# Group 0 of a hybrid decoder step: all v, all u, all q, with four u buffers and later side loads

## The reference, cut to what matters

```python
h = rmsnorm(x, g_mix)
u, q, f, v, og, ga, gb = split(h @ w_in)
# branch A: causal pooling, windows 2, 4, 8, 16 on four groups of 128 channels
pooled = (window_sum(u, w) / count) - u           # one w for each channel group
ya = (pooled @ w_pool * pool_scale) @ w_a
# branch B: gated linear recurrence, 4 heads of 128 x 128
f = lb + (1 - lb) * sigmoid(f);  k = 1 - f
S_t = diag(f_t) S_{t-1} + k_t outer v_t;  o_t = S_t^T silu(q_t)
yb = (rmsnorm(o) * silu(og)) @ w_b
m = sigmoid(ga) * ya + sigmoid(gb) * yb;  x = x + m @ w_out
x = x + relu(rmsnorm(x) @ w_up)^2 @ w_down;  y = rmsnorm(x)
```

## Time and profile before

| | |
|---|---|
| median of 3 runs | 926.98 us (924.71, 926.98, 990.6) |
| the profiled execution | 923.54 us |
| its span, from the first to the last instruction of the slowest core | 922.0 us (core 2) |
| spans of the eight cores | 917.0 to 922.0 us |
| PE busy | 875.5 us, 95% |
| DVE, ACT, POOL busy | 420.2, 360.3, 121.2 us |
| chain that ended last | PE 85%, issue 4%, ACT 3%, DMA 3%, DVE 3%, POOL 2% |
| `arena<-w_in` on that chain | 3% |

### The profile page before, as it was taken

How to read it: one execution, slowest core, us unless ns; L and a number is a source line. 1 busy time by engine, 2 the same in 40 slices (tenths; PEclk the granted TensorE clock), 3 DMA queues, 4 the chain that set the end, 5 groups by cost and what they waited for, 6 DMA issues and landing times.

```text
span 922.0 us, 14969 instructions; the slowest of 8 cores (917.0 to 922.0 us)
## 1 busy us (share of the span) xinstructions
PE 875.5 (95%) x4935; PEld 456.1 (49%) x5017; DVE 420.2 (46%) x692; ACT 360.3 (39%) x636; POOL 121.2 (13%) x190
## 2 busy tenths in 40 slices
PE   4699999999999999999999999999999999999997
PEld 3366754454444434455444444444444444688443
DVE  4555463866757764853643222442134421233122
ACT  4553534666275634652133321332223321333222
POOL 3112420035101430233210000000000000000000
PEclk9799999999999999999999999999999999999999
DMA  9999624047513465996999632400511002200022
GB/s 188 214 156 151 121 86 160 12 132 188 165 55 104 118 168 184 178 150 85 165 212 181 102 92 92 92 1 1 137 49 44 0 4 89 71 2 1 25 68 72
DMA packets 81480, 94.90 MB, mean 103 GB/s; under 512 B 27741, under 2 KB 62173, under 8 KB 81388
## 3 DMA queue, kind: packets, MB, share of 16 engines
q0 software_dynamic: 23984, 30.41, 23.6%
q1 hardware_dynamic: 57420, 63.52, 23.5%
HBM read 92.35 MB, written 26.11 MB: 128 GB/s over the span
## 4 chain that ended last, share of the span: by engine, by line
PE 85%; issue 4%; ACT 3%; DMA 3%; DVE 3%; POOL 2%; DVEq 0%; SPq 0%; ACTq 0%; POOLq 0%
PE ps L585 47%; PE ps L1322 24%; PE ps L597 9%; ACT arena L563 3%; DMA arena<-w_in 3%; PE ps L1028 1%; POOL arena L566 1%; DVE arena L666 1%; DVE arena L566 1%; DMA arena<-meta 1%; PE ps L742 0%; PE ps L880 0%; PE ps L1320 0%; PE ps L619 0%; PE ps L759 0%
## 5 line engine op out<-in xcount | busy, mean ns | idle before, releaser
L585 PE MATMUL ps<-arena 128*128 128x512 bf16 (+2 forms) x2677 | 493.7, 340 | 19.7 <-DMA arena<-w_in 8.0
L585 PEld LDWEIGHTS ps<-arena 128*128 128x128 bf16 x2720 | 262.4, 98 | 226.2 <-issue 29.5
L563 ACT ACTIVATE arena<-ps 128x512 f32<-128x512 f32 (+7 forms) x328 | 191.2, 597 | 307.2 <-PE ps L585 224.2
L563 ACT ACTIVATE arena<-arena 128x1024 bf16<-128x1024 f32 (+7 forms) x235 | 154.3, 669 | 247.8 <-DVE arena L1336 166.9
L1322 PE MATMUL ps<-arena 128*128 128x512 bf16 x1003 | 220.6, 379 | 1.2 <-issue 0.2
L566 DVE TENSOR_TENSOR arena<-arena 128x512 bf16<-128x512 f32 (+6 forms) x214 | 146.8, 692 | 133.4 <-ACT arena L563 125.7
L1322 PEld LDWEIGHTS ps<-arena 128*128 128x128 bf16 x1024 | 100.0, 98 | 121.4 <-issue 1.3
L566 DVE TENSOR_TENSOR arena<-ps,arena 128x512 f32<-128x512 f32 (+5 forms) x155 | 108.4, 716 | 86.2 <-PE ps L585 19.5
L597 PE MATMUL ps<-arena 128*128 128x512 bf16 (+2 forms) x467 | 107.6, 381 | 1.3 <-DMA arena<-w_in 0.4
L1336 DVE SCALAR_TENSOR_TENSOR arena<-ps,arena 128x1024 f32<-128x1024 f32 (+2 forms) x18 | 22.0, 1223 | 152.5 <-PE ps L1322 138.1
L566 POOL TENSOR_TENSOR arena<-arena 128x512 f32<-128x512 bf16 (+7 forms) x78 | 76.0, 982 | 82.6 <-DMA arena<-sth 29.4
(11 more groups left out here) (97 smaller groups left out, 248.4 us busy)
## 6 DMA issues: line engine op xcount, KB each, us to landing
arena<-xp SPq DMA_DIRECT2D x32, 512.0 KB, 6.5
arena<-w_in POOLq DMA_DIRECT2D x9, 1024.0 KB, 23.5
x1d<-arena SPq DMA_DIRECT2D x16, 512.0 KB, 4.9
arena<-w_up POOLq DMA_DIRECT2D x8, 1024.0 KB, 12.7
arena<-x1d SPq DMA_DIRECT2D x16, 512.0 KB, 4.7
y_p<-arena SPq DMA_DIRECT2D x15, 512.0 KB, 3.3
arena<-w_down POOLq DMA_DIRECT2D x5, 1024.0 KB, 24.9
h2d<-arena SPq DMA_DIRECT2D x16, 256.0 KB, 4.1
```

The costliest lines, as they stand in the source:

```text
L563: P.add("act", lambda h: h.activation(out=out, in_=in_, func=func, **kw), reads=reads, writes=writes)
L585: i = h.matmul(ps[:, bb, 0:m], lhsT=wfn(k), rhs=rfn(k, c, m), start=(k == 0), stop=(k == K - 1))
```

## The change

It does five things.

1. In group 0 the twelve units run as v x4, u x4, q x4 (`seq`), where they were v, v, u, v, u, v, q, q, u, q, u, q. Groups 1 to 3 keep the old order.
2. Group 0 has four u buffers; the third and fourth lie on two of the x buffers.
3. The `stp` loads move out of `load_rest1` into `load_rest2` and wait for the eviction of `u_og(0)`. The three early x tiles wait for the load of `w_a` (and for the readers of the third and fourth u buffer). `w_a` goes ahead of ga0 in POOL's queue, and `fold_wa2` goes two units forward, ahead of the last of the first four gb units.
4. The normalisation of the next group's x and the reloads of the present x go 5 later in group 0.
5. Pooling times: in group 0 the third u at 5.1 and 6.1 and the fourth at 6.2 and 7.2 after their units, in groups 1 to 3 the third at 5.5 and 6.5 (was 1.5 and 2.5), the fourth at 4.6 and 5.6 (was 3.2 and 4.1). The recurrence tiles start at 15.6 + 3.35 t, where it was 15.7 + 3.4 t.

```diff
+        r_u += [region(o_x + 4096 * i, 2176) for i in (1, 2)]
+        uext += [view(o_x + 4096 * i, 544, F32) for i in (1, 2)]
@@
         def load_rest1():
             P.add("sp", lambda h: h.dma_start(out=wpf, in_=w_poolT), reads=r_T1[1].bufs, writes=r_wpf.bufs, dma=True)
+
+        def load_rest2():
             for j in range(2):
-                P.add("sp", lambda h, j=j: h.dma_start(out=stp_sb[0:120, j, :], in_=stp[j * 120:(j + 1) * 120, :]), writes=[r_stp.bufs[j]], dma=True)
+                P.add("sp", lambda h, j=j: h.dma_start(out=stp_sb[0:120, j, :], in_=stp[j * 120:(j + 1) * 120, :]), reads=r_sog.bufs[0:1], writes=[r_stp.bufs[j]], dma=True)
@@
-            a, b = ((4.9, 4.9), (3.4, 3.5), (1.5, 2.5), (3.2, 4.1))[gg]
+            a, b = (((5.0, 5.0), (4.6, 4.6), (5.1, 6.1), (6.2, 7.2)) if g == 0 else ((4.9, 4.9), (3.4, 3.5), (5.5, 6.5), (4.6, 5.6)))[gg]
@@
-                    i = m % 2
+                    i = m if g == 0 else m % 2
@@
+                A(19.5, load_rest2)
                 for t in range(3):
-                    A(12.1 + t, lambda t=t: early.update({t: xload(x_rows(1, t), 128, r_T1[3].bufs)}))
-                A(26.2, lambda: [fold_wa2(gg) for gg in range(4)])
+                    A(20.1 + t, lambda t=t: ([activate(r) for r in r_x[1:3]] if t == 0 else None, early.update({t: xload(x_rows(1, t), 128, r_wa.bufs)})))
+                A(24.1, lambda: [fold_wa2(gg) for gg in range(4)])
@@
-                z = 15.7 + e + 3.4 * t
+                z = 15.6 + e + 3.35 * t
@@
-            for fn, i in ((u_v, 0), (u_v, 1), (u_u, 0), (u_v, 2), (u_u, 1), (u_v, 3), (u_q, 0), (u_q, 1), (u_u, 2), (u_q, 2), (u_u, 3), (u_q, 3)):
+            seq = [(u_v, t) for t in range(4)] + [(u_u, m) for m in range(4)] + [(u_q, m) for m in range(4)]
+            for fn, i in seq if g == 0 else ((u_v, 0), (u_v, 1), (u_u, 0), (u_v, 2), (u_u, 1), (u_v, 3), (u_q, 0), (u_q, 1), (u_u, 2), (u_q, 2), (u_u, 3), (u_q, 3)):
@@
-                for t, z in enumerate((7, 11, 14, 17)):
+                for t, z in enumerate((12, 16, 19, 22) if g == 0 else (7, 11, 14, 17)):
@@
-            for t, z in enumerate((13, 16, 19)):
+            for t, z in enumerate((18, 21, 24) if g == 0 else (13, 16, 19)):
```

More of the change, by code:

```diff
@@ L522, in build_program @@
               reads=r_x0[0].bufs, writes=r_w[SLOT["f"]].bufs, dma=True)
-        more = [lambda: load_block("u"), lambda: load_block("q"), lambda: load_block("og"), lambda: load_block("gb0"), lambda: load_block("ga0"),
+        more = [lambda: load_block("u"), lambda: load_block("q"), lambda: load_block("og"), lambda: load_block("gb0"),
                 lambda: P.add("pool", lambda h: h.dma_start(out=wa, in_=w_a.rearrange("(c p) n -> p c n", p=128), max_dma_last_dim=4096), writes=r_wa.bufs, dma=True),
+                lambda: load_block("ga0"),
                 lambda: load_block("ga1"), lambda: load_block("gb1"),
@@ L1087, in group @@
                 U(lambda: u_f(m))
-            for r in r_T2 + r_T3 + r_u + r_pt:
+            for r in r_T2 + r_T3 + r_u[0:4 if g == 0 else 2] + r_pt:
                 activate(r)
@@ L1131, in group @@
                 bN = r_hT[(g + 1) % 2].bufs
-                xl = {}
+                xl = early if g == 0 else {}
                 def pre(t):
```

4 lines of the change are left out of this document (1 added, 3 removed).

## The result

The change made the kernel a little faster, by 0.8%, and more so than forecast: the median is 918.33 us (917.9 to 918.85) against 924.8 for the kernel before beside it. In some runs of some kernels the cores of one die showed a lower granted clock and a longer time, and those runs are left out of every time, ratio and span given here. The ratio is 0.9922, with a 95% interval of 0.9906 to 0.9938. The forecast was 923.7, with a range from 918.5 to 928.0, so the time lies just under the range. The profiled execution took 917.9, its span is 916.4 (922.0 before), and the cores end at 914.6 to 916.4. The slowest is core 7, which ended at 921.2 before.

A forecast was written before the change was run, and what follows sets the result against it. PE bounds the kernel (busy 95%), so only its idle or low-clock time on the last core counts. Core 5: 5.7 won, +3.0 at `a`, +1.2 in groups 1 to 3; span -2.1, time 925.8 to 923.7, range 918.5 to 928.0.

The forecast's parts named there:

- the stage of u and q: Group 0, first f to `meta_state`: q begins at 46.7 on core 2 (gain 8.2), 48.65 on core 5 (gain 5.7).
- The new waits for evictions: Before group 0's first two u units PE waits for ACT's evictions, 0.9 and 0.7 us.
- the rows of core 4: Stretch 30 to 50: core 4's short waits, longest 2.5 us, kept clock 1.00, so new waits cost only their length.
- what cures the wait for u: First u product's 7.1 us wait for weights goes, through new order of units and later loads together.
- u's landing at 35 and q's at 42: Group 0's weight loads: without x tiles and `stp`, u lands at 35 (before 39.2), q near 42 (before 47.3).
- the wait at `a`: Tile 0 of group 0: PE waits 2.4 to 3.0 us for DVE's queue before `a`'s products, taken as +3.0.
- The clock fall behind it: Rival, og units behind group 0's `a`: half speed for a while, costing 2.7, time 926.4; chance 0.2.
- Two rows of other waits: Ground for the clock falling from about 3 us: core 4's 2.5 kept the clock, core 0's 3.2 lost it.
- the low stretch at the fold: Rival, `fold_wa2` and `sample_pool` at 84 to 98: low clock disappears, worth 3.4 us, time 920.4; chance 0.2.
- +0.4 in each group: Groups 1 to 3, around tile 0's `a`: earlier start costs 0.4 per group, 1.2 in all.
- Costed at nothing: `w_a` ahead of ga0 and earlier fold: 0, weights landed by 75; a late block would cost up to 6.75.
- The sum: Whole kernel: core 2 -4.0, but core 5 ends last at 919.9, so the span falls by 2.1 from 922.0.

The follow-up runs named there:

- e3_loads_only: Kernel before with only the later `stp` and x loads, `w_a` ahead of ga0, and group 0's later normalisation and reloads; 918.2 us, ratio 0.9935.
- e5_order_only: Changed kernel with the early `stp` and x loads of before, the two added u buffers on other memory; 921.46 us, ratio 0.9959.
- e10_k6_old_starts: Kernel before plus late loads, `w_a` ahead of ga0, early fold, marker on `w_a`'s load and groups 1 to 3's new pooling; old order, old starts; 912.8 us, 0.9884.
- e1_fold_late: Changed kernel with `fold_wa2` put back in its old place, next to `sample_pool`; 921.6 us, ratio 0.9964.
- e12_marker_only: Changed kernel with only the x tiles waiting for a marker of `w_a`'s load instead of being entered as its readers; 917.95 us, ratio 0.9939.
- e2_groups_old: Changed kernel with the old pooling times and old tile starts in groups 1 to 3; 920.1 us, ratio 0.9952.
- e8_old_starts: Changed kernel with the old tile starts in groups 1 to 3, new pooling times kept; 916.45 us, ratio 0.9917.
- e4_pool3_late: Changed kernel with group 0's third and fourth u pooled later still, behind all `prep_q`; 918.54 us, ratio 0.9937.
- e7_pool3_late_marker: `e4_pool3_late` with the x tiles waiting for a marker of `w_a`'s load instead of being entered as its readers; 913.85 us, ratio 0.9893.
- e9_k7_old_starts: `e7_pool3_late_marker` with the old tile starts in groups 1 to 3; 911.4 and 911.95 us, ratio 0.9871.
- e11_all_old_starts: `e9_k7_old_starts` with the old tile starts in group 0 too; 912.5 us, ratio 0.9876.

## Why the prediction was wrong, step by step

**Right: the stage of u and q.** q was to begin at 46.7 on core 2 and 48.65 on core 5. Counted from the first f, the forecast for `meta_state`'s end was 27.6 on both, and measured is 28.15 plus 0.3. On core 2 the gain is 7.35 (35.49 to 28.14) where 8.2 was forecast. The new waits for evictions were named, in order and place, and under-sized: 1.42 and 1.24 for 0.9 and 0.7. The clock held on all eight cores (PEclk 1.00 over 30 to 50), as the rows of core 4 said. The Trainium skill, TensorE: Matmul & The Clock Gate, "A second HAM failure mode: psum-queue depth-cycling", would have let it fall behind such short waits between PSUM banks. By that rule the trace disagrees in this stage: PEclk was 1.00. In groups 1 to 3, where waits of 1.7 to 1.8 let it fall on some cores and not on others, the trace agrees.

**Right, with its reason only half true: what cures the wait for u.** The forecast gave the cure to order and loads together. `e3_loads_only` gives it to the loads, and `e5_order_only` shows the order curing it on half the cores. The estimates of u's landing at 35 and q's at 42 with SP silent were right: 35.2 and 41.6 on core 2 of the changed kernel. Over its cores u landed between 33.1 and 35.7, and between 34.5 and 41.4 in `e5_order_only`. The Trainium skill, DMA: Bandwidth & Descriptors, "Issuing engines are not separate DMA queues", says that transfers of SP and POOL share the same engines and interleave; the trace agrees, 5.17 of wait for u's load in `e5_order_only` with the x tiles beside it, and none in the same order without.

**Right in size, wrong in its chance: the wait at `a`.** 2.80 was forecast as 2.4 to 3.0, with its cause, DVE's queue. The clock fall behind it was a rival with 0.2 and a price of 2.7. It came on seven of eight cores, for 1.7. Two rows of other waits, at 2.5 and 3.2 us, were too thin a ground for putting the point at 3, and there is no such point: before the first u a wait of 2.88 kept the clock on core 7 of the kernel before, one of 2.32 lost it on core 0 of `e10_k6_old_starts`, and the same 2.80 at `a` lost it on some cores and not on others in every kernel but one.

**Wrong: the low stretch at the fold.** It had a chance of 0.2, "nearly all cores must be spared for the last one to gain". All eight were spared. `e1_fold_late` shows why such a chance is badly reasoned: the eight cores are not eight independent draws. The edit removes the neighbourhood of fold and `sample_pool` on all of them. With the old place the clock fell, fully or for a part, on seven, four and seven of eight cores (the kernel before, `e1_fold_late`, `e3_loads_only`); over 84 to 98 with the new place it is 1.00 on every core of ten kernels. The size, 3.3 to 3.4, was right (63.8 against 60.5).

**Wrong: groups 1 to 3.** The step "+0.4 in each group" was right for the wait at `a` taken by itself (1.50 against 1.10). But it looked at `a` alone, and took the pooling times for an edit whose only effect was there. That is the step whose mechanism failed. The late wait of 1.84 and 1.69, and the fall of the clock behind it, stood in the timeline of before and were not read. Forecast +1.2, measured -1.5, made of -4.8 for the pooling and +3.3 for the starts. Neither size was in the sum.

**Missed, without harm: the x tiles as readers of `w_a`.** "Costed at nothing" held within 0.2 on the core that ends last, but the reason given, that `w_a` lands in time, was not the whole of it.

**The sum.** Forecast for the span -2.1, measured -5.6. Of the 3.5 between them, the fold gives -3.6, groups 1 to 3 give -2.7, and the clock behind `a` gives +1.7. The rest, +1.1, is the stage of u (0.9 longer than forecast, by the longer waits), 0.3 around `a`, less an f that began 0.15 earlier than core 5's had. The two terms put at nothing or with the wrong sign, the fold and the groups, are 6.3 together and fast; the clock at `a` and the longer waits hid 2.8 of it. Each rival was priced alone, and for the groups no gain was in any of them.

**From the span to the time.** The time was missed by 5.4, more than the span. The forecast put it 3.8 above the span, since it started from the mean of two runs, 925.8. The kernel before has 924.8, so 1.0 of the miss is that base. The other 0.9 is that the medians moved by 6.5 and the profiled spans by 5.6, which no edit explains. The time ended 0.2 outside the range. With the base right it would have ended inside, and that would have been luck: the span would still have been forecast to fall by 2.1 and have fallen by 5.6.

## What to carry to other kernels

Price every idle bracket of a repeated stage before pricing an edit in it; here an edit that moved DVE's work moved the waits of PE in the whole stage, and the wait that looked unrelated was the larger. Where an edit on order and an edit on loads both aim at one wait, expect the gain once, and try the loads alone first. To make a transfer wait for another transfer, give the landing a marker of its own: entering the transfer as a reader of the landed buffer makes each later writer of that buffer wait for it.

## What the runs showed of the hardware

- A wait of 2.8 (3.0 on one core) in front of the small matmuls of `a` stands in six kernels with the same instructions there. Behind it the granted clock fell on 36 of their 48 cores: on seven of eight in the changed kernel, six in `e12_marker_only` and `e1_fold_late`, eight in `e2_groups_old`, five in `e8_old_starts`, four in `e5_order_only`. A wait of 0.61 in the same place never did it, on the 24 cores of `e4_pool3_late`, `e7_pool3_late_marker` and `e9_k7_old_starts`.
- Late in groups 1 and 2 stands a wait of 1.7 to 2.2, once in each. With the old pooling times (the kernel before, `e2_groups_old`, `e3_loads_only`) the clock fell behind 24 of 48 such waits, with the new ones and the old starts (`e8_old_starts` to `e11_all_old_starts`) behind 6 of 64. The length of a wait alone does not tell whether the clock falls; what else does is not shown here.
- The price of such a fall was 1.1 to 1.7 (4.44 for 2.75, 7.04 for 5.35), and 2.6 to 2.8 on two cores (8.10 for 5.35 on core 7 of `e2_groups_old`, 7.98 on core 5 of `e5_order_only`).
- The fold's eight matmuls, each 0.38 with 0.22 of idle, followed by 16 float32 matmuls of 120x8, let it fall on four of eight cores in `e1_fold_late`, for up to 3.3. With a gb unit, a ga unit and two recurrence pieces between them it fell on none.
- A block of 1 MB that POOL casts, u's, landed 9.1 to 13.6 us after the block before it with SP's `w_poolT`, `stp` and x tiles beside it, over the cores of the kernel before, and 7.0 to 8.8 after it with only `w_poolT` of these, in the changed kernel. Whether a unit two places later still meets the late block differs from core to core (5.17 of wait on core 0, none on core 1, in `e5_order_only`).
